# Attention steps of TensorE moved into the up and down units of an MLP

## The chip, the core and the metric

The kernel runs on one core of a Trainium2 chip as a single program. The time is the device time of that core in microseconds (us), the median over executions. TensorE (PE) multiplies and transposes, VectorE (DVE) and ScalarE (ACT) read its results out of PSUM, GpSimd (POOL) works on SBUF, SyncE (SP) issues most DMAs. Each engine works through its own instructions in order, and semaphores tie the engines together.

## The reference

One layer of a decoder: normalised input through one combined projection, then two mixers in parallel, one output projection, and an MLP. 2048 prompt tokens and 64 sample tokens go through it. What matters here is the attention of the prompt, in which every block of 128 queries attends to the 256 keys that an indexer chose, and the MLP:

```python
def sparse_attend(q, kg, vg, valid):
    ...
    logits = jnp.einsum('bqngd,bqknd->bqngk', qg, kg.astype(jnp.float32)) * (HEAD_DIM ** -0.5)
    logits = jnp.where(valid[:, :, None, None, :], logits, NEG)
    p = jax.nn.softmax(logits, axis=-1)
    o = jnp.einsum('bqngk,bqknd->bqngd', p, vg.astype(jnp.float32))
...
def residual_block(x, a_o, s_o, w_out, g_post, g_ffn_pre, w_up, w_down, g_ffn_post):
    mix = jnp.concatenate([a_o, s_o], axis=-1) @ w_out
    x = x + rmsnorm(mix, g_post)
    hdn = jnp.square(jax.nn.relu(rmsnorm(x, g_ffn_pre) @ w_up))
    return x + rmsnorm(hdn @ w_down, g_ffn_post)
```

The model width is 1024, the MLP's 4096, with 8 query heads of 64 and 2 key heads. The kernel doesn't gather the chosen keys: it computes all scores up to the block's end and adds a mask.

## The kernel before

The last and longest of the kernel's three parts, `blend`, runs indexer search, attention, output projection and MLP together. At its head a planner writes one list, `plan`, of small units of work. Every engine walks this list in the same order and does its own share of each unit, so the list is the order of all five engines, and semaphores only hold an engine until the data are there.

Units that matter here:

- `("A", s, j)` is one attention step of stage s (four query tiles, 4s to 4s+3). Scores come in banks of 512 keys, so a head of stage s has s+1 banks, and step j stands for bank j. On TensorE the step (`attend_step`) has three parts: the four transposes of the probabilities of bank j (`turn_prob`, line L1691, into `tr`), the two score products of bank j+s+2 (`scores`, L1678 and L1679, into `sc`), and the value products of bank j-2 (`values`, L1700, into `po`). The step at the end of a tile turns its output as well (L1708).
- VectorE's share of a step is to add the mask to the scores of bank j+s+2 and take the running maximum (`mask_scores`, L2381, and with a head's last bank L2387, the negated maximum `nmx`). ScalarE's share is to copy the transposes of bank j-1 to `pT` (`keep_prob`, L1996) and, where bank j+1 begins a head, to raise that whole head (`raise_scores`, L2002). Since a head has s+1 banks, the scores of its last bank are always made in the step before, j-1, and its transposes are the first thing in step j+1. `sc` and `tr` have two PSUM banks each, `pT` three buffers.
- `("U", g, j)` is one up unit: 24 products (`go_up`, L1620) of hidden block j for the 512 tokens of group g, all into one of the three banks of `ring`. Weights and tokens are held in two parts, so each of 8 slices of the sum takes three products: hi by `x_hi`, hi by `x_lo`, lo by `x_hi`.
- `("D", g, m, r)` is a quarter of a down unit: two banks of six products each (`go_down`, L1652) for token tile r.
- The evacuation of a U or D is done by the other engines one feed unit later: `feed_part` of ScalarE, VectorE and POOL begins with `behind(before[u])`. For an up unit that is ScalarE's relu into `hr` (L1907), POOL's square (L2092), ScalarE's high part `h_hi` (L1936) and POOL's low part; for a down bank a copy by ScalarE (L1920) with a sum by POOL (L2111), or a sum by VectorE (L2230). In token group 0 the up and down weights are also split at these units into high part (ScalarE, L1861) and low part (VectorE, L2197); the groups behind it read them ready split from DRAM into the six slots of `ready`, which SyncE fills again as `ring_full` says that a slot's products are done.
- `("S", ...)` are the indexer's search units. W, M, N and E are projection, norms and their like.

The planner merges the stages `S` and `A` of s = 1, 2, 3 into the feed of token groups 0, 1, 2 by cost: an up unit has 5.4, a quarter down unit 2.7, an attention step 0.5. So while a stage attends, nine or ten steps stand behind each up unit and four or five behind each quarter down unit. The steps of stage 0 stand elsewhere, beside the sample tokens' work, and the last group (g = 3) has no steps beside it.

Of the kernel before, what the change touches and what calls it, by code (L numbers as in the profile page):

```python
# [15 lines left out]
D = 1024  # L16
KD = D // P
# [767 lines left out]
def blend(nc, A, ident, par):  # L785
# [87 lines left out]
    plan = [u for u, _ in first_side[:2]] + [("SQ",)] + [u for u, _ in first_side[2:14]]  # L873
# [7 lines left out]
    place = {u: n for n, u in enumerate(plan)}  # L881
# [106 lines left out]
    down_banks = lambda g: [(h, i) for i in tiles_of(g) for h in range(2)]  # L988
# [52 lines left out]
    piece_no, index_bank, n, m = {}, {}, 0, 0  # L1041
# [12 lines left out]
    for s, ts in enumerate(ATTEND):  # L1054
        j = 0
# [7 lines left out]
    m = 0  # L1063
# [17 lines left out]
    with ExitStack() as ctx:  # L1081
# [232 lines left out]
        with nc.Block() as block:  # L1314
# [254 lines left out]
            def _(pe):  # L1569
# [31 lines left out]
                            mm = pe.transpose(x[:, a * P:(a + 1) * P], acc(i)[:, (4 * b + a) * P:(4 * b + a + 1) * P], ident[:])  # L1601
                        mm.then_inc(ring_full, 1)

                def go_up(g, j):
                    if j == 0:
                        pe.wait_ge(free_dve, freed_by[bank_no["N", g, nt(g) - 1, 1]][1])
                    hi, lo = weights(("u", g, j))
                    if both(("U", g, j)):
                        x = bank(("U", g, j, "pair"))[:, 0:2 * P].rearrange("p (c q) -> p c q", c=2)
                        z0 = ready_slot["u", g, j - 1]  # L1610
                        w = ready[:, z0:z0 + 2].rearrange("p c z (k q) -> p z c k q", q=P)
                        for k in range(KD):
                            for z in range(2):
                                mm = pe.matmul(x, XS[:, k], w[:, z, :, k], start=k == z == 0, stop=k == KD - 1 and z == 1)
                        mm.then_inc(ring_full, 1)
                    x = bank(("U", g, j, 0))
                    for k in range(KD):
                        c = slice(k * P, (k + 1) * P)
                        for n, (wt, y) in enumerate(((hi, X[0]), (hi, X[1]), (lo, X[0]))):
                            mm = pe.matmul(x[:], wt[:, c], y[:, k], start=k == n == 0, stop=(k, n) == (KD - 1, 2))  # L1620
                    mm.then_inc(ring_full, 1)
                    if both(("U", g, j)):
                        if j == 1:
                            pe.wait_ge(fold_ok, 1)
                        pe.wait_ge(free_dve, freed_by[bank_no["U", g, j, "pair"]][1])
                        x = bank(("U", g, j, 1))
                        for c in range(2):
                            mm = pe.matmul(x[:, c * NS:(c + 1) * NS], pairs[:, c], fold[:], start=True, stop=True)
                        mm.then_inc(ring_full, 1)
# [4 lines left out]
                        x = bank(("F", g, i, h))  # L1634
                        pe.matmul(x[0:NS, :], fold[:], acc(i)[:, 512 * h:512 * h + 512], start=True, stop=True).then_inc(ring_full, 1)

                def go_down(g, m, r):
                    parts = [weights(("d", g, 2 * m + c)) for c in range(KQ)]
                    pe.wait_ge(h_lo_ok, hid_done(g, 2 * m + 1))
                    for h, i in down_banks(g)[2 * r:2 * r + 2]:  # L1640
                        x = bank(("D", g, m, h, i))
                        tok, col = slice(i * P, (i + 1) * P), slice(512 * h, 512 * h + 512)
                        for c in range(KQ):
                            hi, lo = parts[c]
                            if i == 4:
                                for w in (hi, lo):
                                    mm = pe.matmul(x[:], HS[:, 2 * (m % 2) + c], w[:, col], start=c == 0 and w is hi,
                                                   stop=c == KQ - 1 and w is lo)
                                continue
                            a, b = hid(2 * m + c, 0)  # L1650
                            for n, (f, w) in enumerate(((a, hi), (a, lo), (b, hi))):
                                mm = pe.matmul(x[:], f[:, tok], w[:, col], start=c == n == 0, stop=(c, n) == (KQ - 1, 2))  # L1652
                        mm.then_inc(ring_full, 1)

                def index(s, p, k):
                    ts = SELECT[s]
# [155 lines left out]
                def sample_part(u):  # L1812
# [13 lines left out]
                    elif u[0] == "SO" and u[2] == 1:  # L1826
                        pe.wait_ge(so2_ok, 8 * (u[1] + 1))
                        pe.transpose(ring[0][:, 0:P], o2[:].rearrange("p k d -> p (k d)"), ident[:]).then_inc(st_full, 1)

                pe.wait_ge(ki_ld, 32)  # L1830
                for u in plan:
                    if u == ("AB", 0):
                        pe.wait_ge(kv_res, 96)
                    if u[0] in SAMPLE:
                        sample_part(u)
                    elif u[0] == "S":
                        index(*u[1:])
                    elif u[0] == "A":
                        attend_step(*u[1:])
                    elif u[0] == "W":  # L1840
                        project_out(*u[1:])
                    elif u[0] == "N":
                        turn_x(*u[1:])
                    elif u[0] == "U":
                        go_up(*u[1:])
                    elif u[0] == "D":
                        go_down(*u[1:])
                    elif u[0] == "F":
                        fold_down(*u[1:])

# [774 lines left out]
```

## Time and profile before

| | us |
|---|---|
| median of 3 runs (lowest to highest) | 3652.9 (3649.78 to 3656.28) |
| profiled execution | 3654.93 |
| its span, first to last instruction | 3653.3 |
| TensorE busy (share) | 3051.2 (84%) |
| TensorE weight loads busy | 2407.0 (66%) |
| VectorE busy | 1838.9 (50%) |
| ScalarE busy | 1636.2 (45%) |
| POOL busy | 1262.7 (35%) |

The mean granted TensorE clock is 0.912 of 2.4 GHz over the span. The busy shares are averages over parts of very different kind: projection (to about 400 us), state space, sample tokens and search of stage 0 (to about 1150), then the merged part, and the last token group alone from about 3160 us. The three stretches in which attention steps stand beside up and down units are 1361 to 1509, 1969 to 2206 and 2752 to 3062 us. PE is the row of the products, PEld that of the weight loads, which run ahead of the products. A product's record is longer than the interval to the next one, since they overlap, so intervals are read from start to start. The value products show as 8 records where the program has 4.

### The profile page before, as it was taken

How to read it: one execution, taken by the hardware profiler on the slowest of the kernel's cores; microseconds unless marked ns; L12 is line 12 of the kernel's file. 1: busy time of each engine (PE TensorE's matmuls, PEld its weight loads, DVE VectorE, ACT ScalarE, POOL GpSimd, SP SyncE). 2: the span in 40 equal slices, each digit the busy share in tenths (PEclk: the TensorE clock that was granted, in tenths of full speed). 3: DMA queues.
4: the chain of work that ended last, by engine and by line, in shares of the span. 5: the costliest groups of instructions: out<-in, count | busy, mean ns of one | idle time of the engine just before them, and what ended most of it. 6: DMA issues, size and time to landing. Idle time of an engine off the chain costs nothing.

```text
span 3653.3 us, 46908 instructions
## 1 busy us (share of the span) xinstructions
PE 3051.2 (84%) x15352; PEld 2407.0 (66%) x15352; DVE 1838.9 (50%) x4116; ACT 1636.2 (45%) x2873; POOL 1262.7 (35%) x1181
## 2 busy tenths in 40 slices
PE   7998546557678889997799999869999999799997
PEld 6887432224566668765577886646778888578886
DVE  4333972862357974467785332666772333421112
ACT  3322413612456746575563456746734444322222
POOL 1333621323013551252264114522671112224444
PEclk9999767767889999997899999979999999899999
DMA  4444345636336573353454223343443213544443
GB/s 150 139 145 149 87 129 136 159 117 208 104 138 228 210 244 112 136 215 127 175 186 160 80 72 112 129 177 132 167 174 106 70 61 127 187 149 151 173 150 124
DMA packets 216109, 529.45 MB, mean 145 GB/s; under 512 B 57514, under 2 KB 110828, under 8 KB 189852
## 3 DMA queue, kind: packets, MB, share of 16 engines
q1 hardware_dynamic: 202924, 501.94, 40.4%
q0 software_dynamic: 11360, 22.60, 2.0%
q8 instruction: 125, 2.05, 0.2%
q10 hardware_dynamic: 1584, 1.90, 0.2%
q14 instruction: 116, 0.95, 0.1%
HBM read 399.43 MB, written 134.12 MB: 146 GB/s over the span
## 4 chain that ended last, share of the span: by engine, by line
PE 48%; DVE 12%; issue 11%; ACT 5%; DMA 4%; POOL 4%; SPq 2%; ACTq 0%; POOLq 0%; DVEq 0%
PE r L1620 16%; PE r L1652 12%; PE po L1700 4%; PE tr L1691 3%; ACT junk_a_b L1969 2%; POOL acc_b L2111 1%; PE sc L1679 1%; PE sc L1678 1%; PE r L1809 1%; PE sc L1668 1%; DVE junk_v_b L2350 1%; DVE trial_b L2302 1%; POOL hr_b L2092 1%; PE tr L1668 1%; DVE prob_b L2381 1%
## 5 line engine op out<-in xcount | busy, mean ns | idle before, releaser
L2111 POOL TENSOR_TENSOR acc_b<-acc_b,part_b 128x512 f32<-128x512 f32 x375 | 515.8, 1395 | 494.5 <-ACT part_b L1920 493.6
L1652 PE MATMUL r<-ready_b,h_b 128*128 128x512 f32 x2304 | 565.3, 401 | 44.2 <-ACT part_b L1920 40.2
L1652 PEld LDWEIGHTS r<-ready_b,h_b 128*128 128x128 f32 x2304 | 434.4, 192 | 159.7 <-ACT part_b L1920 52.4
L1620 PE MATMUL r<-x_hi_b,ready_b 128*128 128x512 f32 x1536 | 495.2, 396 | 5.4 <-DVE x_lo_b L2216 2.8
L2092 POOL TENSOR_TENSOR hr_b<-hr_b 128x512 f32<-128x512 f32 x128 | 148.8, 1163 | 780.9 <-ACT hr_b L1907 780.7
L1969 ACT ACTIVATE junk_a_b<-score_b,trial_b 128x384 int8<-128x384 f32 (+13 forms) x266 | 347.5, 1306 | 101.0 <-DVE trial_b L2302 99.9
L1620 PEld LDWEIGHTS r<-x_hi_b,ready_b 128*128 128x128 f32 x1536 | 292.0, 190 | 76.4 <-issue 10.1
L1920 ACT ACTIVATE part_b<-r 128x512 f32<-128x512 f32 x390 | 223.6, 594 | 216.6 <-PE r L1652 127.3
L1620 PE MATMUL r<-x_lo_b,ready_b 128*128 128x512 f32 x768 | 302.0, 393 | 0.0
L1700 PEld LDWEIGHTS po<-V_sb,pT_b 128*128 128x128 f32 x2176 | 286.1, 192 | 23.1 <-issue 3.1
L1996 ACT ACTIVATE pT_b<-tr 128x512 f32<-128x512 f32 (+3 forms) x320 | 168.7, 527 | 264.9 <-PE tr L1691 264.4
L1700 PE MATMUL po<-V_sb,pT_b 128*128 128x64 f32 x2176 | 279.0, 268 | 3.7 <-DVE o_b L2367 3.3
L2381 DVE CUSTOM_DVE_ANT_0 prob_b<-sc,mk_b,mx_b 128x512 f32<-128x512 f32 (+3 forms) x192 | 125.0, 651 | 286.8 <-PE sc L1679 286.4
L2350 DVE TENSOR_SCALAR_CACHE_REDUCE junk_v_b<-score_b,trial_b 128x384 bf16<-128x384 f32 (+13 forms) x182 | 268.2, 1474 | 1.8
L1652 PE MATMUL r<-dn_b,h_b 128*128 128x512 f32 x720 | 188.9, 417 | 42.3 <-ACT part_b L1920 21.0
L2100 POOL TENSOR_TENSOR h_b<-hr_b,h_b 128x512 fp32r<-128x512 f32 x128 | 185.8, 1452 | 96.4 <-ACT h_b L1936 96.4
L2381 DVE CUSTOM_DVE_ANT_0 prob_b<-sc,mk_b 128x512 f32<-128x512 f32 (+3 forms) x128 | 82.1, 642 | 246.3 <-PE sc L1679 177.7
L1691 PE MATMUL tr<-ident_sb,prob_b 128*128 128x128 f32 x1088 | 178.4, 280 | 31.1 <-ACT prob_b L2002 30.2
L1652 PEld LDWEIGHTS r<-dn_b,h_b 128*128 128x128 f32 x720 | 140.2, 200 | 89.3 <-ACT part_b L1920 26.1
L2002 ACT ACTIVATE prob_b<-prob_b,nmx_b 128x128 f32<-128x128 f32 (+15 forms) x128 | 153.9, 1202 | 99.9 <-DVE nmx_b L2387 99.9
L2293 DVE TENSOR_SCALAR turn_b<-count_b 128x1 int32<-128x1 f32 x448 | 68.2, 152 | 249.7 <-ACT junk_a_b L1969 240.4
L1907 ACT ACTIVATE hr_b<-r 128x512 f32<-128x512 f32 x128 | 75.6, 591 | 251.1 <-PE r L1620 251.1
(407 smaller groups left out, 6064.2 us busy)
## 6 DMA issues: line engine op xcount, KB each, us to landing
ready_b<-ws_u SPq DMA_DIRECT2D x96, 1024.0 KB, 6.6
ready_b<-ws_d SPq DMA_DIRECT2D x96, 1024.0 KB, 5.0
ws_u<-up_b SPq DMA_DIRECT2D x32, 1024.0 KB, 9.0
ws_d<-dn_b SPq DMA_DIRECT2D x30, 1024.0 KB, 6.5
kv_b<-kv_pages POOLq DMA_DIRECT2D x128, 128.0 KB, 3.4
kv_b<-kv_pages SPq DMA_DIRECT2D x128, 128.0 KB, 3.1
raw_b<-w_out SPq DMA_DIRECT2D x64, 256.0 KB, 3.4
raw_b<-w_up SPq DMA_DIRECT2D x32, 512.0 KB, 5.5
```

What stands on the lines that cost most here:

```text
L1620: mm = pe.matmul(x[:], wt[:, c], y[:, k], start=k == n == 0, stop=(k, n) == (KD - 1, 2))
L1652: mm = pe.matmul(x[:], f[:, tok], w[:, col], start=c == n == 0, stop=(c, n) == (KQ - 1, 2))
L1691: mm = pe.transpose(x[:, (k - 4 * b) * P:(k - 4 * b + 1) * P], prob[:, n % 2, k * P:(k + 1) * P], ident[:])
L1700: mm = pe.matmul(po[:, h, :], pT[:, prob_no[t, h, b] % 3, k - 4 * b, :], R["V"][:, k, n:n + HD], start=k == 0, stop=k == t)
L1920: act.activation(dst, ring[bank_no[key] % RING][:], ACT.Copy).then_inc(free_act, 1)
L1969: act.activation(junk_a[:, 0:width(t)], score[:, n % 3, 0:width(t)], ACT.Sign, bias=trial[:, 0:1].bitcast(F32), accum_out=count[:, 0:1]).t ...
L1996: act.activation(pT[:, j % 3, 0:m, :], tr[i % 2][:, 0:m * P].rearrange("p (k q) -> p k q", q=P), ACT.Copy).then_inc(tr_free, 1)
L2092: pool.tensor_tensor(s, s, s, ALU.mult).then_inc(sq_ok, 1)
L2100: pool.tensor_tensor(z, s, a.bitcast(F32), ALU.subtract).then_inc(h_lo_ok, 1)
L2111: pool.tensor_tensor(dst, dst, part[:, add_no[key] % 2, :], ALU.add).then_inc(add_pool, 1)
L2350: c.step(dve.tensor_scalar(junk_v[:, 0:width(t)], score[:, turn_s[t] % 3, 0:width(t)], trial[:, lower_trial(t)].bitcast(F32), 0.0, ALU.is_ ...
L2381: dve.tensor_tensor_reduce(out=prob[:, n % 2, 512 * b:512 * b + w], in0=sc[i % 2][:, 0:w], in1=mk[:, t % 2, 512 * b:512 * b + w], scale=1. ...
```

## The change

Only TensorE's order changes. At an up or down unit, TensorE's loop now collects the attention steps that follow it in the plan without another unit in between, and gives them to `go_up` or `go_down`. In `go_up`, steps follow each of the first seven groups of three products, as evenly as the count divides, and the rest come when all 24 are issued and `ring_full` is raised. In `go_down` half the steps (rounded down) follow the first bank, the rest the second. The loop passes over them later. The other engines walk the plan as before.

```diff
--- before.py
+++ after.py
@@ -1601,7 +1601,7 @@
                             mm = pe.transpose(x[:, a * P:(a + 1) * P], acc(i)[:, (4 * b + a) * P:(4 * b + a + 1) * P], ident[:])
                         mm.then_inc(ring_full, 1)
 
-                def go_up(g, j):
+                def go_up(g, j, steps):
                     if j == 0:
                         pe.wait_ge(free_dve, freed_by[bank_no["N", g, nt(g) - 1, 1]][1])
                     hi, lo = weights(("u", g, j))
@@ -1618,7 +1618,12 @@
                         c = slice(k * P, (k + 1) * P)
                         for n, (wt, y) in enumerate(((hi, X[0]), (hi, X[1]), (lo, X[0]))):
                             mm = pe.matmul(x[:], wt[:, c], y[:, k], start=k == n == 0, stop=(k, n) == (KD - 1, 2))
+                        if k < KD - 1:
+                            for step in steps[len(steps) * k // KD:len(steps) * (k + 1) // KD]:
+                                attend_step(*step)
                     mm.then_inc(ring_full, 1)
+                    for step in steps[len(steps) * (KD - 1) // KD:]:
+                        attend_step(*step)
                     if both(("U", g, j)):
                         if j == 1:
                             pe.wait_ge(fold_ok, 1)
@@ -1634,7 +1639,7 @@
                         x = bank(("F", g, i, h))
                         pe.matmul(x[0:NS, :], fold[:], acc(i)[:, 512 * h:512 * h + 512], start=True, stop=True).then_inc(ring_full, 1)
 
-                def go_down(g, m, r):
+                def go_down(g, m, r, steps):
                     parts = [weights(("d", g, 2 * m + c)) for c in range(KQ)]
                     pe.wait_ge(h_lo_ok, hid_done(g, 2 * m + 1))
                     for h, i in down_banks(g)[2 * r:2 * r + 2]:
@@ -1651,6 +1656,9 @@
                             for n, (f, w) in enumerate(((a, hi), (a, lo), (b, hi))):
                                 mm = pe.matmul(x[:], f[:, tok], w[:, col], start=c == n == 0, stop=(c, n) == (KQ - 1, 2))
                         mm.then_inc(ring_full, 1)
+                        half_done = len(steps) // 2 if (h, i) == down_banks(g)[2 * r] else len(steps)
+                        for step in steps[len(steps) // 2 if half_done == len(steps) else 0:half_done]:
+                            attend_step(*step)
 
                 def index(s, p, k):
                     ts = SELECT[s]
@@ -1827,6 +1835,7 @@
                         pe.wait_ge(so2_ok, 8 * (u[1] + 1))
                         pe.transpose(ring[0][:, 0:P], o2[:].rearrange("p k d -> p (k d)"), ident[:]).then_inc(st_full, 1)
 
+                within = set()
                 pe.wait_ge(ki_ld, 32)
                 for u in plan:
                     if u == ("AB", 0):
@@ -1835,16 +1844,20 @@
                         sample_part(u)
                     elif u[0] == "S":
                         index(*u[1:])
-                    elif u[0] == "A":
+                    elif u[0] == "A" and u not in within:
                         attend_step(*u[1:])
                     elif u[0] == "W":
                         project_out(*u[1:])
                     elif u[0] == "N":
                         turn_x(*u[1:])
-                    elif u[0] == "U":
-                        go_up(*u[1:])
-                    elif u[0] == "D":
-                        go_down(*u[1:])
+                    elif u[0] in "UD":
+                        steps = []
+                        for v in plan[place[u] + 1:]:
+                            if v[0] != "A":
+                                break
+                            steps.append(v[1:])
+                            within.add(v)
+                        (go_up if u[0] == "U" else go_down)(*u[1:], steps)
                     elif u[0] == "F":
                         fold_down(*u[1:])
```

TensorE's instructions at an up unit of the second stretch (`r` is the ring bank, `tr`, `sc` and `po` the banks of a step), before: the last 11 of its 24 products, which stand one behind the other, and the first of the nine steps behind them.

```order
L1620 MATMUL r<-x_lo_b,ready_b 128x512
L1620 MATMUL r<-x_hi_b,ready_b 128x512 x2
L1620 MATMUL r<-x_lo_b,ready_b 128x512
L1620 MATMUL r<-x_hi_b,ready_b 128x512 x2
L1620 MATMUL r<-x_lo_b,ready_b 128x512
L1620 MATMUL r<-x_hi_b,ready_b 128x512 x2
L1620 MATMUL r<-x_lo_b,ready_b 128x512
L1620 MATMUL r<-x_hi_b,ready_b 128x512
L1691 MATMUL tr<-ident_sb,prob_b 128x128 x4
L1678 MATMUL sc<-KS_sb,qh_b 128x512
L1679 MATMUL sc<-KS_sb,ql_b 128x512
L1700 MATMUL po<-V_sb,pT_b 128x64 x4
```

The start of the same unit with the change, behind the last step of the unit before (L1699, L1686, L1687 and L1708 are now the lines of L1691, L1678, L1679 and L1700):

```order
L1708 MATMUL po<-V_sb,pT_b 128x64 x4
L1620 MATMUL r<-x_hi_b,ready_b 128x512
L1620 MATMUL r<-x_lo_b,ready_b 128x512
L1620 MATMUL r<-x_hi_b,ready_b 128x512
L1699 MATMUL tr<-ident_sb,prob_b 128x128 x4
L1686 MATMUL sc<-KS_sb,qh_b 128x512
L1687 MATMUL sc<-KS_sb,ql_b 128x512
L1708 MATMUL po<-V_sb,pT_b 128x64 x4
L1620 MATMUL r<-x_hi_b,ready_b 128x512
L1620 MATMUL r<-x_lo_b,ready_b 128x512
L1620 MATMUL r<-x_hi_b,ready_b 128x512
L1699 MATMUL tr<-ident_sb,prob_b 128x128 x4
```

One step now stands between the unit's third and fourth product; the products themselves keep their order and their bank.

TensorE's instructions in the second quarter down unit of the same stretch, before (a step is the four rows tr, sc, sc, po):

```order
L1652 MATMUL r<-ready_b,h_b 128x512 x12
L1691 MATMUL tr<-ident_sb,prob_b 128x128 x4
L1678 MATMUL sc<-KS_sb,qh_b 128x256
L1679 MATMUL sc<-KS_sb,ql_b 128x256
L1700 MATMUL po<-V_sb,pT_b 128x64 x2
L1691 MATMUL tr<-ident_sb,prob_b 128x128 x2
L1678 MATMUL sc<-KS_sb,qh_b 128x512
L1679 MATMUL sc<-KS_sb,ql_b 128x512
L1700 MATMUL po<-V_sb,pT_b 128x64 x4
L1691 MATMUL tr<-ident_sb,prob_b 128x128 x4
```

The same quarter unit with the change (L1657 is now the line of L1652):

```order
L1657 MATMUL r<-ready_b,h_b 128x512 x6
L1699 MATMUL tr<-ident_sb,prob_b 128x128 x4
L1686 MATMUL sc<-KS_sb,qh_b 128x256
L1687 MATMUL sc<-KS_sb,ql_b 128x256
L1708 MATMUL po<-V_sb,pT_b 128x64 x2
L1699 MATMUL tr<-ident_sb,prob_b 128x128 x2
L1686 MATMUL sc<-KS_sb,qh_b 128x512
L1687 MATMUL sc<-KS_sb,ql_b 128x512
L1708 MATMUL po<-V_sb,pT_b 128x64 x4
L1657 MATMUL r<-ready_b,h_b 128x512 x6
L1699 MATMUL tr<-ident_sb,prob_b 128x128 x4
L1686 MATMUL sc<-KS_sb,qh_b 128x512
```

Six of the twelve products moved behind the second step. A head begins at the third step here, the `tr` row right behind them.

## Rows read from the trace of the kernel before

**Rows 1.** Windows view, three attention stretches (us; busy us of each engine; clock; DMA share).
```profile
1361.00:1509.00 148.00, 142.10 (x951) 126.44 (x950) 62.75 (x184) 79.74 (x153) 19.22 (x14) 0.98 0.36 118
1969.00:2206.00 237.00, 224.02 (x1506) 200.34 (x1504) 79.89 (x244) 112.93 (x189) 29.32 (x24) 0.99 0.24 84
2752.00:3062.00 310.00, 294.10 (x2013) 264.60 (x2014) 104.77 (x309) 145.16 (x223) 33.78 (x28) 0.99 0.20 70
```

**Rows 2.** Waits of the weight loads, first stretch (who waits for whom: us, times, longest us).
```profile
PEld tr L1691 <- ACT prob_b L2002: 6.4, 15, 1.6
```

**Rows 3.** The same view, second stretch.
```profile
PEld tr L1691 <- ACT prob_b L2002: 13.0, 20, 1.7
```

**Rows 4.** The same view, third stretch.
```profile
PEld tr L1691 <- ACT prob_b L2002: 15.5, 22, 2.1
...
PEld po L1700 <- ACT pT_b L1996: 1.8, 2, 1.0
PEld r L1652 <- DVE acc_b L2230: 1.8, 3, 1.2
```

**Rows 5.** Timeline, all engines, one wait (start us, us, engine line op, idle before).
```profile
2106.62 0.34 PE L1679 MATMUL sc<-KS_sb,ql_b 128*128 128x384 f32 x1
...
2107.11 0.62 DVE L2381 CUSTOM_DVE_ANT_0 prob_b<-sc,mk_b,mx_b 128x384 f32<-128x384 f32 x1 [0.87 <-PE sc L1679]
...
2107.77 0.15 DVE L2387 TENSOR_SCALAR nmx_b<-mx_b 128x1 f32<-128x1 f32 x1
2107.96 1.47 ACT L2002 ACTIVATE prob_b<-prob_b,nmx_b 128x1408 f32<-128x1408 f32 x1 [0.65 <-DVE nmx_b L2387]
...
2108.21 1.00 PE L1700 MATMUL po<-V_sb,pT_b 128*128 128x64 f32 x8
...
2109.57 0.66 PE L1691 MATMUL tr<-ident_sb,prob_b 128*128 128x128 f32 x4 [0.36 <-ACT prob_b L2002]
```

**Rows 6.** Timeline of PE, into and out of an up unit.
```profile
2092.53 1.00 PE L1700 MATMUL po<-V_sb,pT_b 128*128 128x64 f32 x8
2093.34 0.47 PE L1620 MATMUL r<-x_hi_b,ready_b 128*128 128x512 f32 x1
2093.66 0.40 PE L1620 MATMUL r<-x_lo_b,ready_b 128*128 128x512 f32 x1
2093.89 0.62 PE L1620 MATMUL r<-x_hi_b,ready_b 128*128 128x512 f32 x2
...
2098.68 0.40 PE L1620 MATMUL r<-x_hi_b,ready_b 128*128 128x512 f32 x1
2098.92 0.60 PE L1691 MATMUL tr<-ident_sb,prob_b 128*128 128x128 f32 x4
...
2099.81 1.00 PE L1700 MATMUL po<-V_sb,pT_b 128*128 128x64 f32 x8
2100.65 0.61 PE L1691 MATMUL tr<-ident_sb,prob_b 128*128 128x128 f32 x4
```

**Rows 7.** Timeline of PE, into and out of a down unit.
```profile
2060.37 1.00 PE L1700 MATMUL po<-V_sb,pT_b 128*128 128x64 f32 x8
...
2064.03 0.60 PE L1691 MATMUL tr<-ident_sb,prob_b 128*128 128x128 f32 x4
```

**Rows 8.** Timeline, odd up unit of the first stretch.
```profile
1380.89 0.48 PE L1620 MATMUL r<-x_hi_b,up_b 128*128 128x512 f32 x1
...
1383.70 1.22 DVE L2197 TENSOR_TENSOR up_b<-raw_b,up_b 128x1024 fp32r<-128x1024 f32 x1
...
1383.89 0.26 ACT L1996 ACTIVATE pT_b<-tr 128x128 f32<-128x128 f32 x1
```

**Rows 9.** Timeline, odd up unit of the second stretch.
```profile
2028.42 0.59 ACT L1907 ACTIVATE hr_b<-r 128x512 f32<-128x512 f32 x1
...
2029.79 0.48 PE L1620 MATMUL r<-x_hi_b,ready_b 128*128 128x512 f32 x1
...
2030.70 0.58 ACT L1996 ACTIVATE pT_b<-tr 128x512 f32<-128x512 f32 x1
```

## The prediction

> **What bounds the kernel now.** I read the windows view first, over the three stretches in which attention steps stand in the plan beside up and down units: 148, 237 and 310 us, 695 of the 3653.3 us span [rows 1]. The reader is to see that TensorE's products are busy there for 94 to 96% of the time at a granted clock of 0.98 or 0.99, while VectorE and ScalarE are about half idle. TensorE's own queue sets the time, and the change touches nothing else. Products overlap in the records, so I looked for lost time where the next weights are loaded, in the waits of the weight loads: 6.4, 13.0 and 15.5 us, 34.9 us in 57 waits, are spent ahead of `turn_prob` until ScalarE's exp (L2002) is done [rows 2 to 4]. The third stretch has 3.6 us more, in waits for a copied transpose and for VectorE's sum of a down bank [rows 4]. So the change can win some 38 us at the most, 1% of the span.
>
> One such wait, step by step [rows 5]. Step j-1 issues the last scores of a head (ql, 2106.62). VectorE masks them (2107.11), finds the maximum (2107.77), ScalarE raises them (2107.96, 1.47 us), and the transposes of that head, first thing in step j+1, start at 2109.57, 2.95 us after the scores. In between TensorE has only the values of step j-1 and the whole of step j. The wait is what is left: value products to transposes take 1.36 us here (2108.21 to 2109.57) against 0.84 where nothing is waited for (2099.81 to 2100.65 [rows 6]), 0.52 lost, each time that a head begins at the third step of a group or later.
>
> **The change, part by part.** No instruction is added, removed or resized. Nine or ten steps that followed the 24 products of an up unit now stand one behind each three products, two behind the last three; four or five steps behind a down unit's 12 products stand two behind the first six, the rest behind the last six. In the plan 55 groups of steps follow such a unit: 17 of nine or ten, 32 of four or five, 6 of one or two.
>
> *Waits that go.* What decides is whether products stand between step j-1 and the transposes of step j+1. Counted from the plan, of the 96 heads of these stretches 67 have none between them before, and 8 after: 14 get three products, 74 six. The 8 left begin at the fifth step of a down unit. Three products are 3 x 0.228 = 0.68 us (0.228 from 2093.89 to 2098.68, 21 intervals [rows 6]), six 1.37 us. The mean wait is 34.9 / 57 = 0.61 us, so three products cover most, six all but the first heads of stretches two and three (some 1.0 us left, since these wait 1.7 and 2.1 us now [rows 3, 4]). Left: 8 x 0.61 + 1.0 = 5.9 us; gone: 29.0. Of the 3.6 us of other waits I take 3.0 as gone, since the unit's products now stand among the steps that wait.
>
> *Breaks that come.* TensorE goes from steps into products 208 times instead of 55, 153 times more. Such a break has a price, and the trace has it [rows 6]: value products to the first up product 0.81 us, that to the second 0.32, the second to the third 0.23, the last one to the transposes 0.24 us. That is 1.60 us for three products with their entry and exit; without the break the value products run into transposes in 0.84 us, and three products take 0.68. So 0.08 us. For the 24 products as a whole: 6.39 us from 2092.53 to 2098.92, less 0.84 and 24 x 0.228, is 0.08; a down unit (2060.37 to 2064.03 [rows 7]) 3.66 - 0.84 - 12 x 0.228 = 0.08. Bounds: nothing, if short bursts hide the wide first product; and 0.18 us, if an interval like the first (0.32 against 0.23) also falls on the second product, at the exit too. I take 0.10, near the rows and a little over, for 15.3 us.
>
> The Trainium skill ("TensorE: Matmul & The Clock Gate", Step-by-step: what each phase is for) says that TensorE pulls the next weight load ahead of the product that runs and that products then follow at their streaming time, whatever stood before. By that a break is free and the term of 15.3 us is zero; the rows above show 0.08 us at the seams, so the measurement decides for the forecast, and the rule is the third rival.
>
> *ScalarE's and VectorE's unit work that loses its cover.* Their order keeps each unit's own work (relu, splits, h_hi, sums) ahead of its steps. Until now the 5.5 us of up products covered it; now the second step comes 0.79 + 1.73 + 0.79 = 3.3 us after the unit's start (three products and their exit, a full step from 2098.92 to 2100.65, three products again [rows 6]), and needs ScalarE's copy of the last transposes of the group before. In stretches two and three ScalarE starts that copy 0.91 us after the unit (2029.79 to 2030.70 [rows 9]); only where an exp of about 2 us stands before or behind it does it come late, by some 0.3 us. I count 2 us for the nine units of these stretches in which a head begins at the first or second step and ScalarE also waits for POOL's square. In the first stretch the weights are still split: an odd up unit starts at 1380.89, the copy comes at 1383.89 and VectorE's second split runs from 1383.70 for 1.22 us, so to 4.0 us after the start [rows 8]; then mask, maximum and exp (about 1.5 us) set the third step's transposes to 5.6 us instead of 4.9. With two odd up units and two down units behind them, 3 us. Together 5 us. Queued behind are only later steps of the same stretch: POOL has no step work, and SyncE's reload of a slot, which waits for an up bank that is now full seven steps, some 12 us, later, is for a piece used a whole round of up and down units later.
>
> Sum: -29.0 - 3.0 + 15.3 + 5.0 = -11.7 us. Nothing behind these stretches has slack of its own, since the search, the feed and the last layer group follow on TensorE's order, so I let all of it through: 3654.9 - 11.7 = 3643.2 us for the profiled execution, which lies 2.0 us above the median of the three runs shown; against that median 3641.2, say 3641 us.
>
> **The rivals.** *The gain is eaten (no change).* The break costs its upper bound of 0.18 us, 27.5 us in all, or the lost cover costs 15 us instead of 5. Then -32 + 27.5 + 5 = +0.5, or -32 + 15.3 + 15 = -1.7: about 3652 us. For it: the gain is a difference of terms of like size. Against it: three seams in rows 6 and 7 all give 0.08 us.
>
> *Slower: ScalarE is late at the second step.* Now it starts a unit's relu 1.4 us before TensorE starts the unit (2028.42 against 2029.79 [rows 9]). If the denser order brings it to the unit 1.5 us later, the copy, and an exp behind it, end after the second step wants them in each of the 16 units of these stretches that need POOL's square first, at some 2 us a time, and the next down units inherit it: 32 us, so -32 + 15.3 + 32 = +15.3, 3668 us. It decides from about 1 us of wait in each of the 16. Against it: ScalarE idles half of each stretch [rows 1].
>
> *Free breaks.* If seams overlap in short bursts, -29.0 - 3.0 + 5.0 = -27 us: 3626 us. For it: at a break TensorE always has the operands ready. This is what the skill's rule gives. Against it the same rows 6.
>
> **How the numbers follow.** Forecast 0.48, eaten 0.25, slower 0.14, free breaks 0.13. The forecast's own range is 3633 to 3649 us (breaks at 0.05 to 0.14 us each, cover at 3 to 7 us). What a measurement can tell from no change is about 0.2%, 7.3 us, so faster means below 3645.6: 0.41 of the forecast and the free breaks, 0.54; no change 0.07 of the forecast and 0.23 of the eaten gain, 0.30; slower 0.16. The range of 3629 to 3662 us leaves out half of the free breaks and most of the slower case.
>
> **What would show it.** In the profile after: the waits of weight loads for exp in the three stretches down from 34.9 to 6 to 9 us; product to product 0.23 us inside a three and value products to first product 0.81, with 0.32 behind it; the stretches shorter by up to 2, about 5 and about 6 us. Waits for ScalarE's copy (L1996) ahead of second steps, summing over 10 us, would make the cover term wrong; an unchanged wait for exp would make the first term wrong; a seam over 0.18 us the second. A lower granted clock in the stretches would upset all of it.

## The result, and the profile after

| | before | after |
|---|---|---|
| median, us (lowest to highest) | 3652.9 (3649.8 to 3656.3) | 3625.0 (3621.7 to 3629.9) |
| span of the profiled execution | 3653.3 | 3625.8 |
| granted clock over the span | 0.912 | 0.915 |

The ratio is 0.9925, 95% interval 0.9907 to 0.9942: faster by 27.9 us, where 11.7 were forecast, and below the range of 3629 to 3662 us. Two later comparisons of the same kernel gave 0.9938 and 0.9942, so 21 to 27 us; the mean of the three ratios is 24 us. Set on the 3652.9 us of this table, the two later ratios give 3630 and 3632 us, just inside the range: that the first time fell below it is partly chance, that the gain is about twice the forecast is not.

The windows view of the changed kernel, over the same three stretches (columns as in [rows 1]):

```profile
1360.60:1505.50 144.90, 142.04 (x957) 125.91 (x956) 64.45 (x184) 81.40 (x154) 18.81 (x15) 0.98 0.37 121
1967.90:2195.00 227.10, 220.86 (x1507) 196.52 (x1505) 79.98 (x244) 112.36 (x189) 29.30 (x24) 1.00 0.26 88
2740.00:3036.00 296.00, 292.45 (x2009) 261.68 (x2010) 104.04 (x309) 146.12 (x224) 35.09 (x29) 0.99 0.22 75
```

The work is the same to a few records, the stretches are 3, 10 and 14 us shorter, and products fill 97 to 99% of them. The waits of the weight loads in the same order of stretches (us, times, longest; they answer [rows 2 to 4]), first stretch:

```profile
PEld tr L1699 <- ACT prob_b L2015: 2.4, 4, 0.8
PEld po L1708 <- ACT pT_b L2009: 2.1, 2, 1.2
```

second:

```profile
PEld tr L1699 <- ACT prob_b L2015: 3.9, 7, 0.9
...
PEld tr L1716 <- DVE o_b L2380: 0.5, 1, 0.5
```

third:

```profile
PEld tr L1699 <- ACT prob_b L2015: 3.4, 5, 1.4
...
PEld po L1708 <- ACT pT_b L2009: 1.8, 2, 1.0
```

34.9 us in 57 waits for exp have become 9.7 us in 16. In the third stretch the wait for VectorE's sum of a down bank is gone; the two waits for ScalarE's copy of a transpose stand as before, 1.8 us. The head of [rows 5], all engines, in the changed kernel:

```profile
2096.34 0.33 PE L1687 MATMUL sc<-KS_sb,ql_b 128*128 128x384 f32 x1
...
2096.82 0.62 DVE L2394 CUSTOM_DVE_ANT_0 prob_b<-sc,mk_b,mx_b 128x384 f32<-128x384 f32 x1 [1.60 <-PE sc L1687]
...
2097.09 0.48 PE L1620 MATMUL r<-x_hi_b,ready_b 128*128 128x512 f32 x1
...
2097.66 1.47 ACT L2015 ACTIVATE prob_b<-prob_b,nmx_b 128x1408 f32<-128x1408 f32 x1 [0.65 <-DVE nmx_b L2400]
...
2099.48 0.47 PE L1620 MATMUL r<-x_hi_b,ready_b 128*128 128x512 f32 x1
...
2100.26 0.60 PE L1699 MATMUL tr<-ident_sb,prob_b 128*128 128x128 f32 x4
```

From scores to transposes there are now 3.92 us instead of 2.95, filled with two times three products (from 2097.09 and 2099.48), and the transposes show no idle time before them. The seams, where [rows 6] had them only at the ends of 24 products:

```profile
2084.64 1.00 PE L1708 MATMUL po<-V_sb,pT_b 128*128 128x64 f32 x8
2085.45 0.47 PE L1620 MATMUL r<-x_hi_b,ready_b 128*128 128x512 f32 x1
2085.76 0.40 PE L1620 MATMUL r<-x_lo_b,ready_b 128*128 128x512 f32 x1
2086.00 0.40 PE L1620 MATMUL r<-x_hi_b,ready_b 128*128 128x512 f32 x1
2086.23 0.60 PE L1699 MATMUL tr<-ident_sb,prob_b 128*128 128x128 f32 x4
```

0.81, 0.31, 0.24, 0.23 us from start to start: as forecast (0.81, 0.32, 0.23, 0.24), and the interval behind the first product is longer than 0.23, so a break isn't free.

**A measure that the clock doesn't disturb.** The same scores product (L1678, now L1686) ends each group of steps behind a unit in both kernels. The time from one such start to the next, group by group, is a ledger of the change. It repeats: of 42 groups away from the start of a stretch, 39 differ by 0.03 us or less over three profiles of the changed kernel, and the other three by 0.04 to 0.07. Together these 42 are 19.6, 19.8 and 19.7 us shorter than before. The ledger ends where a stretch runs out of scores products: there the last one itself moved to an earlier place within its unit (behind 6 of the 12 products of a down unit, behind 3 of the 24 of an up unit), so the interval shrinks by 1.37 or 4.78 us without a gain, and such groups don't count. What moves by whole microseconds from one execution to the next is the rest: at ScalarE's relu of the last up unit ahead of the first stretch, before anything is changed, the thirteen other profiles of this study stand between 6.0 us earlier and 5.8 later than the kernel before.

### The profile page after: what moved, and what is told of

It is laid out like the page before. It is cut to its first block, busy times and chain, and to the rows that moved or that the text cites. A ratio compares the mean times of both kernels' runs of the same rounds, so it can differ in the third digit from the quotient of the medians.

```text
span 3625.8 us, 46903 instructions
## 1 busy us (share of the span) xinstructions
PE 3036.5 (84%) x15347; PEld 2396.8 (66%) x15352; DVE 1840.4 (51%) x4116; ACT 1637.7 (45%) x2873; POOL 1262.6 (35%) x1181
## 4 chain that ended last, share of the span: by engine, by line
PE 50%; DVE 11%; issue 9%; ACT 5%; DMA 4%; POOL 4%; SPq 2%; ACTq 0%; POOLq 0%; DVEq 0%
PE r L1620 16%; PE r L1657 12%; PE po L1708 6%; PE tr L1699 3%; ACT junk_a_b L1982 2%; PE sc L1686 2%; PE sc L1687 2%; POOL acc_b L2124 1%; PE sc L1676 1%; DVE junk_v_b L2363 1%; PE r L1817 1%; POOL hr_b L2105 1%; DVE trial_b L2315 1%; PE tr L1676 1%; PE r L1586 1%
## 5 line engine op out<-in xcount | busy, mean ns | idle before, releaser
L1657 PE MATMUL r<-ready_b,h_b 128*128 128x512 f32 x2304 | 574.4, 403 | 41.5 <-ACT part_b L1933 38.3
L1657 PEld LDWEIGHTS r<-ready_b,h_b 128*128 128x128 f32 x2304 | 434.2, 193 | 155.5 <-ACT part_b L1933 51.1
L1620 PE MATMUL r<-x_hi_b,ready_b 128*128 128x512 f32 x1536 | 516.5, 400 | 5.4 <-DVE x_lo_b L2229 2.8
L1708 PEld LDWEIGHTS po<-V_sb,pT_b 128*128 128x128 f32 x2176 | 286.7, 191 | 23.4 <-ACT pT_b L2009 4.5
L1708 PE MATMUL po<-V_sb,pT_b 128*128 128x64 f32 x2176 | 279.2, 268 | 3.7 <-DVE o_b L2380 3.3
L1657 PE MATMUL r<-dn_b,h_b 128*128 128x512 f32 x720 | 189.8, 417 | 42.4 <-ACT part_b L1933 21.1
L1657 PEld LDWEIGHTS r<-dn_b,h_b 128*128 128x128 f32 x720 | 138.9, 199 | 88.7 <-ACT part_b L1933 26.2
L1699 PE MATMUL tr<-ident_sb,prob_b 128*128 128x128 f32 x1088 | 174.2, 275 | 11.5 <-ACT prob_b L2015 10.6
```

Of the source, the lines that this page charges most:

```text
L1699: mm = pe.transpose(x[:, (k - 4 * b) * P:(k - 4 * b + 1) * P], prob[:, n % 2, k * P:(k + 1) * P], ident[:])
L1708: mm = pe.matmul(po[:, h, :], pT[:, prob_no[t, h, b] % 3, k - 4 * b, :], R["V"][:, k, n:n + HD], start=k == 0, stop=k == t)
```

## The experiments

**The changed kernel once more, twice.**

> The changed kernel once more, unaltered, for the question how much of its 27.9 us comes from outside the three stretches, where the instructions are the same in both kernels. In its first profile the stretches gained 3.5, 10.1 and 13.6 us; between the first and second 2.8 us were given back, where TensorE ran at half clock from about 1509 to 1519 us, and 3.4 us were won behind the third, also at another length of half clock. If those differences belong to one execution and change from one to the next: stretches again 3.5, 10 and 13.6 us to within 0.5, and the parts outside different by some us, total 3622 to 3630. If they belong to the order of the kernel: +2.8 and -3.4 us at the same places again.

> The changed kernel unaltered, beside the run that mixes the two ways of cutting, on the same chip. Groups of steps without half clock as in both earlier profiles to within 0.02 us each; between the stretches other lengths of half clock. Median between its two earlier ones, 3625.0 and 3632.4, since the groups are the same and only the parts between them vary.

Measured: 3632.4 us (ratio 0.9938, 0.9924 to 0.9951) and 3635.0 us (0.9942, 0.9926 to 0.9959), both slower than expected. U(0,19) is the up unit of hidden block 19 of token group 0. How much longer (+) or shorter (-) it takes from ScalarE's relu of one up unit to that of another, against the first profile of the kernel before, us; in the last two columns kernels whose order isn't changed in that part (experiments below):

```
part                            after  again  again2 | third_only before_busy
start of program to U(0,19)      -0.4   +3.0    +5.8 |   -6.0       +3.6
U(0,19) to U(0,23)  stretch 1    -3.5   -4.0    -3.9 |   +2.4       +3.4
U(0,23) to U(1,17)  between      +2.8   +0.5    +0.1 |   +0.7       +0.7
U(1,17) to U(1,23)  stretch 2   -10.1   -9.8   -10.0 |   -3.0       -3.0
U(1,23) to U(2,21)  between      +0.5   -0.7    +0.1 |    0.0       -1.1
U(2,21) to U(2,29)  stretch 3   -13.6  -11.0   -11.0 |  changed     +1.1
U(2,29) to U(3,0)   behind       -3.4   -2.9    +0.3 |   +0.5       -1.9
```

The parts between are chance of one execution (+2.8, +0.5, +0.1), as the first of the two readings said, but the third stretch gave 11.0 us and not 13.6 again: its groups agree, and most of the difference, 2.3 us, stands ahead of the first of them. The stretches of the first profile of before were not typical either: a kernel with the same order there takes 2.4 to 3.4 us more in the first stretch and 3.0 less in the second. Against these other profiles the change is worth about 6.7, 6.9 and 13 us (the third against one profile, +1.1); with the first profile of before counted in, 5.7, 7.9 and 12.4: some 26 us either way. Two or three profiles are few for this: the first group of the first stretch alone stands 1.4 us below to 2.7 above the kernel before in profiles in which its order is unchanged. The windows view shows what moves there, in the first profile after, between stretches one and two:

```profile
1505.00:1510.00 5.00, 2.93 (x9) 1.61 (x8) 0.00 (x0) 0.00 (x0) 1.29 (x1) 0.88 0.33 105
1510.00:1515.00 5.00, 5.00 (x11) 2.34 (x10) 0.95 (x2) 2.67 (x6) 0.00 (x0) 0.50 0.01 3
1515.00:1520.00 5.00, 5.00 (x15) 3.88 (x14) 3.27 (x2) 1.70 (x3) 2.52 (x2) 0.59 0.05 6
```

At a granted clock of 0.50 (1.2 GHz) TensorE issues 11 products in 5 us; the kernel before issues 23 from 1515 to 1520, at 1.00:

```profile
1515.00:1520.00 5.00, 5.00 (x23) 3.45 (x20) 1.13 (x3) 3.93 (x8) 1.57 (x2) 1.00 0.02 3
```

**Up units alone, down units alone.** In the first, all steps of a down unit stand behind it; in the second, all steps of an up unit:

```diff
 up_only, go_down:
-                        half_done = len(steps) // 2 if (h, i) == down_banks(g)[2 * r] else len(steps)
-                        for step in steps[len(steps) // 2 if half_done == len(steps) else 0:half_done]:
-                            attend_step(*step)
+                    for step in steps:
+                        attend_step(*step)
```

> Only the up units take their steps between the products; the steps of a down unit stand behind it as before. Theory A (read from both traces, group of steps by group): waits of transposes for exp behind up units go (19.3 us before, some 0.5 left), two waits for the normalised output go (2.2 us), the 119 further breaks cost 0.07 to 0.08 us each (9 us), and no cover is lost: -12 to -14 us, so 3639 to 3641 against 3653. Theory B, the prediction's prices: 18.5 us of waits go, breaks at 0.10 us are 11.9 us, lost cover 4 us: -3 us, 3650.

> Only the down units take their steps between the two banks; the steps of an up unit stand behind it as before. Theory A: of 17.4 us of waits for exp behind down units 6.6 stay (heads at the fifth step, and the starts of stretches two and three), a wait for the output (1.1) and one for VectorE's sum (1.7) go, the starts of stretches two and three win some 2 us more because their first scores come six products earlier, 32 breaks cost 2.5 us: -13 us, and 3640. Theory B, the prediction's prices: 11 us of waits and 1.7 us of others go, breaks 3.2, cover 1: -8.5 us, 3644. Together with the run of the up units alone: the two gains add up to that of the changed kernel to within 2 us if nothing couples them.

Measured: 3638.7 us (0.9952, 0.9939 to 0.9966) and 3639.0 us (0.9954, 0.9940 to 0.9967), against 3654.7. Both agree with theory A and not with the prediction's prices (3650, 3644). In the ledger, away from the starts of stretches, each group behaves in them as in the kernel that has both changes, to 0.1 us (behind up unit 20 of group 1, -0.73, -0.74 with up units alone and 0.00 with down units alone): nothing couples the two. The two gains add up to 34 us by the ratios, more than the 24 of the whole change, where 2 us of difference were expected. Each ratio is uncertain by 1.3 parts in a thousand, 5 us, and the 42 groups show no such excess: 9.6 and 10.5 us, against 19.6 to 19.8 together.

**No exp wait at all, in both orders.** In stages 1 to 3 the transposes read the identity instead of the probabilities; VectorE then waits for exp itself before it writes the buffer:

```diff
-                    pe.wait_ge(prob_ok, n + 1)
+                    if t < 4:
+                        pe.wait_ge(prob_ok, n + 1)
...
-                        mm = pe.transpose(x[:, (k - 4 * b) * P:(k - 4 * b + 1) * P], prob[:, n % 2, k * P:(k + 1) * P], ident[:])
+                        mm = pe.transpose(x[:, (k - 4 * b) * P:(k - 4 * b + 1) * P], prob[:, n % 2, k * P:(k + 1) * P] if t < 4 else ident[:], ident[:])
...
+                        if t >= 4:
+                            dve.wait_ge(prob_ok, n - 1)
```

> The kernel before, in its own order, but in stages 1 to 3 the transposes turn the identity instead of the probabilities, so that TensorE never waits for exp there (VectorE waits for exp itself before it writes a buffer of probabilities again). Leaves out that the probabilities reach the values. Theory A: the term of the exp waits is what the records show, 36.8 us of lengthened intervals ahead of transposes (34.9 in the list of waits), and nothing takes their place: -35 to -38 us, 3616. Rival: other waits behind them (ScalarE's copy of the transposes, which stands behind exp on ScalarE, and VectorE's mask) take half their place: 3634.

> The changed order, with the transposes of stages 1 to 3 turning the identity instead of the probabilities (leaves out that the probabilities reach the values). Beside the same of the kernel before (3616.7 us) no exp wait is left in either, so the difference is the breaks, any lost cover, and the few other waits. Theory A: 153 further breaks at 0.075 us are 11.5 us, cover costs nothing, the waits for the output and for VectorE's sum (5 us) go: about +6.5 us, 3623; by group of steps, +0.05 to +0.09 us for each further break, nothing else. Theory B, the prediction's prices: 15.3 + 5 - 3 us, about +17, 3634. Free breaks: -5 us, 3612.

Measured: 3616.7 us (0.9894, 0.9879 to 0.9910) and 3622.7 us (0.9918, 0.9897 to 0.9938). Theory A had 3616 and 3623. The group behind up unit 20 of token group 1 shows both terms: it runs from one of these rows to the next, in the kernel before (21.03 us),

```profile
2091.99 0.48 PE L1678 MATMUL sc<-KS_sb,qh_b 128*128 128x512 f32 x1
...
2113.02 0.48 PE L1678 MATMUL sc<-KS_sb,qh_b 128*128 128x512 f32 x1
```

before without exp waits (19.89 us),

```profile
2080.64 0.48 PE L1678 MATMUL sc<-KS_sb,qh_b 128*128 128x512 f32 x1
...
2100.53 0.48 PE L1678 MATMUL sc<-KS_sb,qh_b 128*128 128x512 f32 x1
```

the changed kernel (20.30 us),

```profile
2084.09 0.48 PE L1686 MATMUL sc<-KS_sb,qh_b 128*128 128x512 f32 x1
...
2104.39 0.48 PE L1686 MATMUL sc<-KS_sb,qh_b 128*128 128x512 f32 x1
```

and the changed kernel without exp waits (20.31 us):

```profile
2073.75 0.48 PE L1686 MATMUL sc<-KS_sb,qh_b 128*128 128x512 f32 x1
...
2094.06 0.48 PE L1686 MATMUL sc<-KS_sb,qh_b 128*128 128x512 f32 x1
```

Its two waits cost 1.14 us (the list of waits gives them 1.0). The changed order wins all of that back (20.30 against 20.31) and pays 0.42 for seven breaks: 0.060 us each. Nine of the eleven up groups that the ledger has in stretches two and three, this one among them, pay 0.41 to 0.45 for seven. The other two pay 0.84 and 0.76; in both TensorE also waits 0.6 us for ScalarE's copy of a transpose. A down group pays 0.03 to 0.10 for one break, mostly 0.04 to 0.06, where no other wait changed.

**Cuts only where a head needs them.** A chunk of products is put ahead of a head's first transposes only if the head begins at the third step of the group or later and the chunk before doesn't cover it, 67 cuts in place of 153:

```diff
+                def cuts_of(steps, parts):
+                    at, last = [], 1
+                    for q, (s, j) in enumerate(steps):
+                        if (s, j) in bank_of and bank_of[s, j][2] == 0 and q > last:
+                            at.append(q)
+                            last = q + 1
+                    n = len(at) + 1
+                    return [(parts * (i + 1) // n, q) for i, q in enumerate(at)]
```

> A unit's products are cut only where a head's first transposes stand at the third step of the group or later and the products before don't cover them: 67 cuts in place of 153, each chunk three products or more, up and down units alike (the heads at the fifth step of a down unit, which still wait in the changed kernel, now have products before them). Theory A: 86 fewer breaks at 0.075 us save 6.5 us, the waits that were left (8.9 us, of which some 2 at the starts of stretches stay) save 6: -12 us against the changed kernel, -37 against before, about 3616. Rival: the unit's bank is full later and other engines' work behind it collides with the next heads, so that waits for ScalarE's copy or VectorE's mask take back half: 3622. By the prediction's prices: -8.6 - 6 + nothing, 3613.

> The kernel with aimed cuts once more, unaltered, to see whether it and the mixed one differ. By the groups of steps, half clock left out, it is 2 us behind the mixed kernel in the first stretch and 1 ahead in the second. If the groups decide: a ratio to the kernel before of 0.992 to 0.993, as the mixed kernel. If its first ratio of 0.991 was its own: again 0.991, 3620 us.

Measured: 3622.9 us (0.9911, 0.9893 to 0.9928) and 3625.4 us (0.9923, 0.9909 to 0.9936), so 28 to 33 us faster than before and some 6 faster than the changed kernel, not 12. The second is inside what the groups promised. The ledger says where the rest stayed. Heads at the fifth step of a down unit are covered now, seven of the eight with 0.5 to 0.9 us each, and four to six breaks fewer in an up group give 0.2 to 0.35. But waits came back: 0.5 and 0.9 us in two up groups of the first stretch (the 0.5 behind a down group that is itself 0.9 us shorter), 0.8 in one down group, and at the last tile of every stretch that for the normalised output, which the even cuts had hidden but for 0.5 us in the second (second stretch; the third has the same row of 1.0):

```profile
PEld tr L1736 <- DVE o_b L2400: 1.0, 1, 1.0
...
PEld tr L1719 <- ACT prob_b L2035: 0.3, 1, 0.3
```

**Both ways mixed.** Even cuts in the up units of the first stretch and in those in which a tile's output is turned, aimed cuts elsewhere:

```diff
+                    if g == 0 or any(tile_at(*step[:1], step[1] - 4) is not None for step in steps):
+                        cuts = [(k, len(steps) * k // KD) for k in range(1, KD)]
```

> Down units, and the up units of stretches two and three, are cut only at heads, as in the run with aimed cuts; the up units of the first stretch and those in which a tile's output is turned are cut after every three products, as in the changed kernel, since the aimed cuts brought waits back there. By the groups of steps of the earlier traces, the best of both in each: 34 us won in the stretches and 2 at their ends, against 27 and 2 in the changed kernel: 7 us less than the changed kernel, -33 to -36 us against before, 3619 to 3621. Rival: what a group wins comes back in the next one (as at the first down group of a later round, where the aimed cuts lost 0.8 us), so no more than the aimed cuts gave: 3623.

Measured: 3626.5 us (0.9927, 0.9913 to 0.9941), against 3635.0 of the changed kernel on the same chip, 8.5 us less, where 7 were expected. Against the kernel before it is 27 us and not the 33 to 36 expected, no better than the aimed cuts, and which of the two is best isn't settled.

**ScalarE's cover.** The relu of each up unit with steps behind it runs three times, in the order before and in the changed one:

```diff
+                            for _ in range(2 if plan[place[u] + 1][0] == "A" else 0):
+                                act.activation(s, x, ACT.Relu).then_inc(twice_ok, 1)
...
+                                act.wait_ge(twice_ok, twice[0])
                             act.activation(s, x, ACT.Relu).then_inc(free_act, 1)
```

> The kernel before, with ScalarE's relu of an up unit that has steps behind it done three times over (same result), some 1.3 us more on ScalarE at the start of each of 19 units. It shows how much of ScalarE's unit work is covered when 24 products stand ahead of the first step. Expected by both theories: covered nearly whole, 0 to +3 us, 3654 to 3657.

> The changed kernel with the same threefold relu, 1.3 us more of ScalarE at each of 19 up units, now with three products ahead of the first step. If the prediction was right that the cover is about used up (copy some 0.3 us late behind an exp already), each unit pays most of the 1.3 us: +15 to +25 us on the changed kernel's 3628, 3643 to 3653. If ScalarE has slack between the unit and the second step, as the groups without waits say (+0.05 us for a group with one break): +0 to +5 us, 3628 to 3633.

Measured: 3654.9 us (0.9995, 0.9986 to 1.0005) and 3646.5 us (0.9979, 0.9968 to 0.9991). Behind 24 products the extra work is free. Behind three it is not: by the ledger 12 us more than the changed kernel, by the ratios 16. That is about the lower end of the first expectation (15 to 25) and far from the second (0 to 5), but it isn't paid at each unit: ten groups pay 0.7 to 1.3 us each. Each stands at a unit at whose start ScalarE does the relu (an odd up unit, or the first down unit of a round) and has a head at its first or second step; groups without both pay nothing, and neither do two down groups of the first stretch that have both. In one of the ten, ScalarE is late and the transposes wait for its copy:

```profile
2107.97 0.60 ACT L1927 ACTIVATE hr_b<-r 128x512 f32<-128x512 f32 x1
...
2109.72 0.63 ACT L1956 ACTIVATE h_b<-hr_b 128x512 fp32r<-128x512 f32 x1 [1.15 <-POOL hr_b L2112]
2110.25 0.96 ACT L2016 ACTIVATE pT_b<-tr 128x384 f32<-128x384 f32 x2
...
2110.87 0.63 PE L1700 MATMUL tr<-ident_sb,prob_b 128*128 128x128 f32 x4 [1.10 <-ACT pT_b L2016]
```

**The third stretch alone.**

```diff
+                        if u[1] != 2:
+                            (go_up if u[0] == "U" else go_down)(*u[1:], [])
+                            for step in steps:
+                                attend_step(*step)
+                            continue
```

> Steps stand among products in the third stretch only (token group 2); the first two are as before. If nothing behind a stretch has slack, the 13.5 us that the groups of the third stretch won, and 0.8 at its end, reach the end of the kernel, give or take the half clock behind it: -11 to -17 us, 3637 to 3643. If the gain of a stretch were given back to a wait behind it, the last token group would start at its old time: 3654.

Measured: 3642.6 us (0.9969, 0.9959 to 0.9980). The stretch is 11.2 us shorter in the table above's terms, 10.7 of them are there at the first up unit of the last token group and at its last. What a stretch wins reaches the end.

## Why the prediction was wrong

The direction and the mechanism held; both terms that cost time, the breaks and the lost cover, were sized too high, and the waits that go too low. By its own steps:

- **Waits for exp: nearly right.** 29.0 us were to go and 5.9 to stay. All of them are worth 38 us by the medians (the kernel before without them, interval 33 to 44), so the ceiling of 38 us that the prediction set for all waits together was low. 5.9 us stay (the 42 groups of the changed kernel with and without them), so about 32 went, uncertain by the 5 us of the ratio. The groups by themselves, without the starts of stretches, had 31.0 us and lost 25.1. One reason for the difference is that the list of waits, from which 34.9 came, falls short of what the intervals lose: 1.0 for 1.14 us in the group above, 0.8 for 0.92 in another, 1.7 for 1.84 in a third. The prediction had the better measure in its hands, the interval from value products to transposes in [rows 5, 6], and used it only as an illustration.
- **Breaks: the first failed step.** "I take 0.10, near the rows and a little over, for 15.3 us." The ledger gives 0.06 us in up units (120 breaks) and mostly 0.04 to 0.06 in down units (33), about 9 us in all. The rows themselves said 0.08; rounded to 0.01 us each, four intervals of one seam can carry an error of about 0.02, which here is multiplied by 153. And the step from 0.08 to 0.10 rested on nothing. The third rival's mechanism, free breaks, is false all the same (0.42 us for seven), although its 3626 us is what was first measured: several errors of one sign met its number by luck. The rule of the Trainium skill ("TensorE: Matmul & The Clock Gate", Step-by-step: what each phase is for), as the prediction applied it to breaks, would have been wrong by 9 us, my price by 6.
- **Lost cover: the second failed step.** 5 us were taken. The ledger of the changed kernel against the same without exp waits shows it in the first two up groups of the first stretch (0.7 us in the second; the first begins the stretch and isn't clean). Beyond its breaks, an up group of the second stretch pays 0.4 us for a wait for ScalarE's copy: 1 to 2 us in all, of which I take 1. The mechanism is real, as the threefold relu shows, but ScalarE is done just in time. The prediction had 3 us for the first stretch and 2 us for nine units of the others, where the work ends at the very moment it is wanted and costs nothing. The slower rival, ScalarE late by 1 us in 16 units, would have needed the extra 1.3 us of that experiment, and even then it stayed faster than before.
- **Other waits: too low, and in part the wrong ones.** 3.0 of the 3.6 us in [rows 4] were counted, and between 5 and 6 went, of which I take 5. Of those 3.6, the half for ScalarE's copy didn't go at all: 1.8 us in 2 waits before and after. The wait for VectorE's sum went (1.5 us in one down group of the third stretch, with and without exp waits). Not counted were three waits for the normalised output at the ends of stretches, 1.0 us each in the list, of which 0.5 us is left in the second, and 0.2 to 0.6 us in each of four other groups, 1.7 us in all (read from the two kernels without exp waits).
- **Nothing behind has slack: right**, as the third stretch alone shows.
- **Two slips that decide nothing.** The bounds given for the forecast's own range (breaks at 0.05, cover at 3 us) sum to -21.3 us, so 3632 and not 3633. And VectorE, said to be about half idle, is idle for 58 to 66% of the stretches [rows 1].

So -32 + 9 + 1 - 5 = -27 us, where -29 + 15.3 + 5 - 3 = -11.7 was forecast, and -24 is measured (-21 to -27). Of the 15 us between the two sums, 10 are costs put too high, and 5 are waits put too low: every uncertain term was rounded toward no gain. The signs that the prediction named came as it said: waits for exp at 9.7 us, a little over its 6 to 9, seams as forecast, and no 10 us of waits for the copy. The stretches alone stood against it, 6.7, 6.9 and 13 us shorter where up to 2, 5 and 6 were named.

Left open: whether the ratios of the changed kernel really fall, from 27 to 21 us in three comparisons (their intervals overlap), while its ledger doesn't move. The parts outside the ledger vary by more than that between executions, but their mean wasn't measured.

## What to carry to other kernels

When one engine sets the time and waits for a chain through others at known places, put its independent work just there; even cuts of three products won 24 us, and cuts only where a chain is longer than its cover, less than half as many, some 6 more. A small cost that is multiplied by a hundred is to be averaged over many seams in the trace and not padded, and a stall is to be priced by the interval from start to start of the same instructions, which the list of waits understates by about a tenth. Give the helper engines the same look: work that three products just cover is free, and 1.3 us more of it was paid for in ten places.

## What the hardware showed beyond that

In these traces the granted clock of TensorE goes to its lower level, 1.2 GHz, for some microseconds where a stage begins behind a stall (here the products behind a wait of 2.07 us for a DMA at 1508.6 us, granted 0.50 from 1510 to 1515), and when and for how long it does varies between executions: between U(0,23) and U(1,17) the changed kernel took 2.8, 0.5 and 0.1 us more than the one profile of before in three profiles. Away from such places the intervals of 42 groups of steps, 8 to 24 us long, repeat to 0.03 us in all but three, on different chips. Fourteen single profiles spread by 12 us ahead of the first changed instruction, so a change of 0.3% can be read in a ledger of groups where it can't be in one span.
